# Wider spacing of the normed input's tiles, and a smaller DMA scratch area

## The reference

```
for layer in range(DEPTH):
    x = x + 0.5 * swiglu(rmsnorm(x, norm_gain[layer, 0]), gate, up, down)   # D_FF = 2816
    h = rmsnorm(x, norm_gain[layer, 1])
    if layer % 2 == 0:
        x = x + conv_sparse_attn_mixer(h, cos, sin, w_in, conv_w, w_out, top_k)
    else:
        x = x + gated_deltanet_mixer(h, w_in, conv_w, a_log, dt_bias, o_gain, w_out)
    x = x + 0.5 * swiglu(rmsnorm(x, norm_gain[layer, 2]), gate, up, down)
return rmsnorm(x, final_gain)
```

## Time and profile before

| | us |
|---|---|
| median of 3 runs | 2073.67 (2073.62 to 2074.37) |
| span of the profiled execution | 2072.4 |
| PE busy in it | 2052.6 (99%), 9592 matmuls |
| PEld busy | 1704.6 (82%) |
| DVE busy | 1025.5 (49%) |
| ACT busy | 779.5 (38%) |
| POOL busy | 305.1 (15%) |
| DMA moved | 199.02 MB, mean 96 GB/s |

### The profile page before, as it was taken

The page is one execution under the profiler, slowest core; times in us unless marked ns, Lnnn a source line. Parts: engine busy times, 40 slices in busy tenths (PEclk is TensorE's granted clock), DMA queues, the critical chain, the costliest instruction groups (busy, mean ns, idle before and its releaser), DMA issues.

```text
span 2072.4 us, 25759 instructions
## 1 busy us (share of the span) xinstructions
PE 2052.6 (99%) x9592; PEld 1704.6 (82%) x9592; DVE 1025.5 (49%) x1540; ACT 779.5 (38%) x1110; POOL 305.1 (15%) x390
## 2 busy tenths in 40 slices
PE   9999999999999999999999999999999999999998
PEld 7888888788888888888888888878888888888887
DVE  5444444488644444432444443266776544444423
ACT  5333322346743333322333322265565553333222
POOL 1000000354220000000000000047566010000000
PEclk9999999999999999999999999999999999999999
DMA  5323322354132333322333332223122132333331
GB/s 182 101 91 101 114 98 83 109 137 127 51 92 92 98 94 99 115 93 83 88 100 96 97 118 98 69 89 93 58 83 89 62 92 91 101 92 100 112 98 55
DMA packets 63100, 199.02 MB, mean 96 GB/s; under 512 B 12816, under 2 KB 14896, under 8 KB 63024
## 3 DMA queue, kind: packets, MB, share of 16 engines
q1 hardware_dynamic: 59616, 196.55, 30.3%
q10 hardware_dynamic: 3408, 1.44, 0.3%
HBM read 188.51 MB, written 2.38 MB: 92 GB/s over the span
## 4 chain that ended last, share of the span: by engine, by line
PE 92%; DVE 3%; ACT 2%; POOL 1%; issue 1%; DMA 1%; SPq 0%; ACTq 0%; DVEq 0%; POOLq 0%
PE prod L510 27%; PE prod L512 27%; PE prod L511 27%; PE misc L777 2%; PE misc L723 1%; PE prod L574 0%; PE prod L575 0%; PE prod L578 0%; ACT L1215 0%; PE misc L657 0%; PE misc L713 0%; PE prod L700 0%; POOL rows L1797 0%; PE prod L622 0%; PE prod L623 0%
## 5 line engine op out<-in xcount | busy, mean ns | idle before, releaser
L1275 DVE TENSOR_TENSOR w_lo<-raw,w_hi 128x1024 fp32r<-128x1024 f32 (+1 forms) x290 | 383.2, 1321 | 737.6 <-ACT w_hi L940 737.1
L510 PE MATMUL prod<-h_hi,w_hi 128*128 128x512 f32 x1848 | 737.9, 399 | 2.6 <-DVE w_lo L1275 1.2
L512 PE MATMUL prod<-h_hi,w_lo 128*128 128x512 f32 x1848 | 721.2, 390 | 0.0
L511 PE MATMUL prod<-h_lo,w_hi 128*128 128x512 f32 x1848 | 720.1, 390 | 0.0
L940 ACT ACTIVATE w_hi<-raw 128x1024 fp32r<-128x1024 f32 (+1 forms) x316 | 354.8, 1123 | 542.8 <-PE prod L512 527.2
L510 PEld LDWEIGHTS prod<-h_hi,w_hi 128*128 128x128 f32 x1848 | 347.6, 188 | 74.8 <-issue 6.4
L512 PEld LDWEIGHTS prod<-h_hi,w_lo 128*128 128x128 f32 x1848 | 347.1, 188 | 73.9
L511 PEld LDWEIGHTS prod<-h_lo,w_hi 128*128 128x128 f32 x1848 | 347.8, 188 | 68.1 <-issue 1.7
L510 PE MATMUL prod<-a_hi,w_hi 128*128 128x512 f32 x682 | 265.3, 389 | 0.0
L511 PE MATMUL prod<-a_lo,w_hi 128*128 128x512 f32 x682 | 265.3, 389 | 0.0
L512 PE MATMUL prod<-a_hi,w_lo 128*128 128x512 f32 x682 | 265.3, 389 | 0.0
(11 more groups left out here) (306 smaller groups left out, 1860.7 us busy)
## 6 DMA issues: line engine op xcount, KB each, us to landing
raw<-in_w SPq DMA_DIRECT2D x252, 512.0 KB, 3.6
raw<-in_wd SPq DMA_DIRECT2D x64, 704.0 KB, 4.1
blk<-blocks SPq DMA_DIRECT2D x16, 256.0 KB
x<-in_x SPq DMA_DIRECT2D x8, 256.0 KB, 6.0
k_dup<-k_dup SPq DMA_DIRECT2D x8, 256.0 KB, 3.7
silu_g<-g_rows SPq DMA_DIRECT2D x7, 256.0 KB, 4.7
out<-y_out SPq DMA_DIRECT2D x12, 128.0 KB, 1.8
raw<-in_w SPq DMA_DIRECT2D x4, 256.0 KB, 6.1
```

The lines of the kernel that those rows point to most:

```text
L510: pe.matmul(bank, wh, hi, start=first and k == 0, stop=False)
L511: pe.matmul(bank, wh, lo, start=False, stop=False)
L512: ins = pe.matmul(bank, wl, hi, start=False, stop=last and k == tiles_n - 1)
L1275: dve.tensor_tensor(w_lo[:, n % 2, 0:w], raw[:, n % 4, 0:w], w_hi[:, n % 2, 0:w].bitcast(F32), ALU.subtract).then_inc(lo_ready, 1)
```

## The change

Two lines and a constant. `h_hi` is allocated 576 values wide for a tile and `h_lo` 520, and a slice takes the first 512 of each, so that the tiles lie 2304 and 2080 bytes apart. The 64 and 8 values between are neither written nor read. The program is built with a DMA scratch area of 8192 bytes of each partition, where the default is 16384. No instruction is added, removed or moved; addresses differ.

```diff
+H_HI_PAD, H_LO_PAD = 64, 8
...
         x = sb("x", [KT, T])
         h_at = (nc.sbuf_base + 31) // 32 * 32
-        h_hi, h_lo = sb("h_hi", [KT, T], F32R), sb("h_lo", [KT, T], F32R)
+        h_hi, h_lo = sb("h_hi", [KT, T + H_HI_PAD], F32R)[:, :, 0:T], sb("h_lo", [KT, T + H_LO_PAD], F32R)[:, :, 0:T]
...
-    nc = bacc.Bacc("TRN2", target_bir_lowering=False, num_devices=1)
+    nc = bacc.Bacc("TRN2", target_bir_lowering=False, num_devices=1, dynamic_dma_scratch_size=8192)
```

## The result

The changed kernel takes 2095.87 us, the median of 3 runs (2095.79 to 2096.56), against 2073.67 before: 22.2 us more, ratio 1.0109 (95% interval 1.0091 to 1.0127). The forecast was 2073.7 us, within 0.2%. It is slower than the range's upper end, 2083, and than the dearer form of rival B, 2091. The profiled execution has a span of 2094.1 us, 21.7 over the 2072.4 of before.

A forecast was written before the change was run, and what follows sets the result against it. PE was taken as the bound, busy 99% of the span. With every part of the change at 0 us, 2072.4 + 0 + 1.3 (median over this execution's span) gave 2073.7 us, range 2048 to 2083 us.

The forecast's parts named there:

- rival B: Matmuls on h_lo tiles starting off the 256-byte grid pay: 2082.5 us, or 2091 if the next matmul pays too; chance 0.16.
- The bound: Whole kernel: PE, busy 99% of the span and 92% of the chain that ended last, sets the time.
- the price of the spacing: In the 5712 matmuls that stream h, new tile spacing costs 0 ns each, 0 us in all.
- Its sign: The slower case would show at L578, on h_lo, as over 1.58 us for the seven matmuls in a row.
- its count: Of 1904 matmuls streaming h_lo, 7/8 start off the 256-byte grid and pay: 1666, or twice the cost if the next pays.
- The price of 5.3 ns: Extra over the plain step, from five delta mixer matmuls taking 232 ns each; over 1666 matmuls 8.8 us.
- Rival A: In matmuls on h, new spacing frees the fixed cost: 1998 us if all, 2048 us if every third; chance 0.19.
- The fixed 13.3 ns: What each matmul costs beside its columns, 226.7 ns less 512 x 0.417; freed from 5712 matmuls, 76 us less.
- The writes of h: ACT's 723 ns and DVE's 750 ns tile writes of h_hi and h_lo stay the same: 0 us.
- the shift: Everything behind h moves down by 5888 bytes, keeping mutual distances, so the down projections stay as they are: 0 us.
- the scratch: The DMA scratch area that is cut is used by nobody, all DMAs running on hardware_dynamic queues: 0 us.
- the clock: PE's clock is 2.4 GHz in plain stages, lower around the delta mixer's pause; 2 us allowed either way.

The follow-up runs named there:

- e2_hi_only: The changed kernel with only h_hi padded (tiles 2304 bytes apart) and h_lo back at 2048: 2074.41 us, ratio 1.0001 to the kernel before.
- e4_lo_2304: The changed kernel with h_lo padded by 256 bytes too, both tensors' tiles 2304 bytes apart: 2073.39 us, ratio 1.0000 to the kernel before.
- e3_lo_only: The changed kernel with only h_lo padded (tiles 2080 bytes apart) and h_hi back at 2048: 2096.44 us, ratio 1.0107 to the kernel before.
- e7_gap32: The changed kernel without pads, but with 32 bytes left free between h_lo and raw, ahead of the weights: 2104.53 us, ratio 1.0151 to the kernel before.
- m2_pairs: Kernel without the decoder, groups of 32 matmuls with starts moved in pairs, singly or in the kernel's pattern: 7.42 us plain, 7.58 with low tiles moved by 32 k.
- e1_scratch_only: The changed kernel with both pads at zero, so only the scratch is 8 KB: 2074.08 us, ratio 1.0001 to the kernel before.
- m1_offsets: Kernel without the decoder, 45 groups of 32 matmuls with tile or weight starts moved constantly, alternating or stepping: 7.42 us plain, 7.61 with tiles 32 bytes off.

## Why the prediction was wrong

**The bound** was right. PE holds the end, and what happened, happened in its step.

**The step that failed is the price of the spacing, taken as 0 ns for each matmul.** I had noted that all tiles and weights of the trace begin on one residue modulo 512 bytes and that a dependence finer than this would be new, and then let the regular rows weigh as if they spoke of it. They couldn't. The rows showed that steps of 512, 2048 and 16384 bytes are alike; the runs showed that 256 is too (e2_hi_only, e4_lo_2304), and that 32 isn't (e3_lo_only).

The trace of before held a warning that I passed over. Rows 4 to 6 show one step, but in the mixers the same matmuls on h stood at other steps without any padding. From one matmul on h to the next it was 229.1 ns on average in the attention mixer and 230.4 in the delta mixer. I used five of them as a price and not as evidence that the step varies.

**Rival B** named the right part, the low tiles off the 256-byte grid. Its sign, over 1.58 us for the seven matmuls on `h_lo`, came with 1.63. Two things in it were wrong. Its condition was the tile's own start; it is the distance to the weights (e7_gap32: 31.3 us with every tile where it was). And its count, 1666 matmuls or twice that, was too small. In a unit every one of the 24 matmuls pays on average, `h_hi`'s as well, since the cost of one disturbed matmul is spread over some ten. Its 2091 us lies near the 2095.87 measured, but with a wrong condition and a wrong count this is in part luck. The price of 5.3 ns, read off the delta mixer, was near the 5.0 measured. 5712 x 5.0 is 28.6 us; the 22.2 measured are less mostly by what the mixers don't pay. There the step on h went only from 229.1 to 232.0 and from 230.4 to 231.0 ns. In the changed kernel five of the delta mixer, at a like place, take the 1.15 us below; the five of before took 1.16.

```profile
1487.24 0.39 PE L512 MATMUL prod<-h_lo,w_hi 128*128 128x512 f32 x1
...
1488.39 0.38 PE L787 MATMUL prod<-q_dec,state 128*128 128x128 f32 x2
```

That the small fp32 matmuls between the tiles leave the same kind of aftermath, and that the row I took as a price for disturbance was this very effect, fits both rows and the 0.1 us of the delta mixer. The single steps fit too. Behind such fp32 matmuls, from 1470.56 us in the trace of before, they are 235, 233, 236, 224 and 232 ns. The plain group of m2_pairs that follows the moved pairs settles by 228, 235, 233, 236, 224 and 231 ns. No run isolated it in the mixer.

**Rival A** fell. The fixed 13.3 ns are not freed by spreading the starts; in the scan of 64 distances, with 512 columns, they are the least.

**The writes of h, the shift, the scratch and the clock** were right: DVE and ACT keep their times, a's step is 226.7 ns, and e1_scratch_only stands at 1.0001. The granted clock is 0.998 on average in both traces.

The Trainium skill (TensorE: Matmul & The Clock Gate, "Step-by-step: what each phase is for") says that loading the next weights takes no SBUF read bandwidth from the running matmul, since each has its own read port. The runs show that where the weights lie isn't indifferent to the running matmul: the distance between the two starts moves the step from 226.7 to 240.0 ns, for fp32r operands and 512 columns. Whether it is read bandwidth that goes lost, no run shows. The same page's N / 2.4 plus 2.5 ns, 215.8, given for a matmul by itself, was reached in no group.

**What stays open** is the mechanism. The runs show a fixed, irregular dependence on the distance modulo 256 bytes and an aftermath. Why a change that keeps the distance costs something in the next seven matmuls, and why an alternation by 192 bytes costs nothing, is open. Whether the weights of the same matmul or of the next one count was not settled, and why 28 bytes are plain and 32 aren't has no explanation here.

## What to carry to other kernels

Where TensorE is the bound and the operands are fp32r with 512 columns, keep the starts of streamed tiles and of weights on one residue modulo 256 bytes: pad rows by multiples of 64 values or not at all, and look at what stands between two allocations, since 32 free bytes cost 1.5% here. A regular trace is evidence only for the relations that occur in it. When a change leaves the grid on which all of them lie, the answer isn't in the trace, and the chance of a price should be set accordingly.

## What the runs showed of the hardware that I had not expected

- The settled step of an fp32r matmul of 512 columns lies between 226.7 and 240.0 ns, set by the distance between the streamed tile's start and the weights' start modulo 256 bytes; both moved alike settle back to plain.
- A disturbance repeats to the nanosecond: the first low tiles of the changed kernel (from 377.32 us) take 227, 236, 232, 231, 237, 232 and 236 ns, and so do the first seven matmuls of m1_offsets' group that steps by 32 bytes (L134).
- One matmul off by 32 or 64 bytes costs 54 or 47 ns in all by the starts, spread over about ten matmuls; off by 128 bytes it costs some 7 ns and leaves nothing behind.
- With 256 columns an offset of 32 bytes is faster: 32 matmuls in 3.94 us instead of 4.00, some 2 ns each. With plain fp32 operands there is no difference, 27.63 us for 64 passes both times.
